# First projection of a two-layer encoder: units in pairs, square sums moved, second weight tile loaded earlier

## The reference, cut to what matters

```python
h = rms_norm(x, g_pre)                       # x * rsqrt(mean(x*x) + EPS) * g
proj = jnp.einsum('btd,de->bte', h, w_in)    # D = 1024 -> 2976 columns
qa, ka, va, cq, ckv, kr, gate = jnp.split(proj, SPLIT_AB, axis=-1)
```

## Time and profile before

| | |
|---|---|
| median of 3 runs | 2136.87 us (2136.51 to 2137.25) |
| profiled execution | 2129.73 us, span 2127.9 us |
| busy share: PE, PEld, DVE, ACT, POOL | 96%, 76%, 61%, 53%, 45% |
| DMA | 260.29 MB, 122 GB/s mean |

### The profile page before, as it was taken

The page is one execution under the profiler, slowest core; times in us unless marked ns, Lnnn a source line. Parts: engine busy times, 40 slices in busy tenths (PEclk is TensorE's granted clock), DMA queues, the critical chain, the costliest instruction groups (busy, mean ns, idle before and its releaser), DMA issues.

```text
span 2127.9 us, 25150 instructions
## 1 busy us (share of the span) xinstructions
PE 2041.6 (96%) x9334; PEld 1626.7 (76%) x9334; DVE 1287.6 (61%) x1922; ACT 1122.3 (53%) x1420; POOL 953.1 (45%) x477
## 2 busy tenths in 40 slices
PE   7999998999999999999997999999999999998997
PEld 5878876788888877777785777887777777775775
DVE  6232135326777766674568677524577887788454
ACT  7142234335666666664456444243677777777431
POOL 1222234334555555555001666423566666766401
PEclk9999999999999999999998999999999999999999
DMA  5133468527665555454335233261333333332534
GB/s 188 45 129 131 149 242 319 152 75 151 129 125 115 109 118 114 90 178 151 91 107 180 94 109 109 89 194 66 82 69 66 75 79 75 77 110 84 168 101 157
DMA packets 167434, 260.29 MB, mean 122 GB/s; under 512 B 75456, under 2 KB 84288, under 8 KB 167312
## 3 DMA queue, kind: packets, MB, share of 16 engines
q1 hardware_dynamic: 167312, 258.68, 42.5%
HBM read 160.72 MB, written 97.91 MB: 122 GB/s over the span
## 4 chain that ended last, share of the span: by engine, by line
PE 82%; DVE 10%; ACT 3%; issue 2%; DMA 2%; POOL 0%; SPq 0%; DVEq 0%; ACTq 0%
PE SA L1847 11%; PE OP L1891 9%; PE SA L473 5%; PE OP L473 5%; PE SM L1773 5%; PE OP L998 5%; PE SA L998 4%; PE OP L1898 4%; PE SM L1946 4%; PE SA L1946 3%; PE OS L473 3%; PE OS L1891 2%; PE OS L998 2%; PE SM L1769 2%; PE OS L1946 2%
## 5 line engine op out<-in xcount | busy, mean ns | idle before, releaser
L2295 POOL TENSOR_TENSOR c_PL<-c_PF,c_PH 128x1024 fp32r<-128x1024 f32 x128 | 308.8, 2418 | 151.8 <-ACT c_PH L2023 82.0
L2295 POOL TENSOR_TENSOR ab_PL<-ab_PF,ab_PH 128x1024 fp32r<-128x1024 f32 (+3 forms) x128 | 266.6, 2085 | 189.0 <-ACT ab_PH L2023 130.8
L2020 ACT ACTIVATE ab_PF<-SA 128x1024 f32<-128x1024 f32 (+3 forms) x160 | 143.6, 898 | 157.9 <-PE SA L1808 83.1
L2100 DVE TENSOR_REDUCE c_MH<-SM 128x1 f32<-128x512 f32 x256 | 171.8, 686 | 75.6 <-PE SM L1773 74.9
L2020 ACT ACTIVATE c_PF<-SA 128x1024 f32<-128x1024 f32 x160 | 164.0, 1025 | 93.7 <-PE SA L1847 93.3
L394 POOL TENSOR_TENSOR e_wl<-e_raw,e_wh 128x1024 fp32r<-128x1024 f32 (+1 forms) x31 | 73.6, 2375 | 217.7 <-ACT e_wh L539 217.7
L2023 ACT ACTIVATE c_PH<-c_PF 128x1024 fp32r<-128x1024 f32 x128 | 135.7, 1061 | 4.1
L1847 PE MATMUL SA<-c_Q,c_KA 128*128 128x512 f32 x320 | 129.4, 404 | 7.9 <-ACT c_PF L2020 7.9
L1773 PE MATMUL SM<-c_KA,c_Q 128*128 128x512 f32 x320 | 126.8, 398 | 4.4 <-DVE c_MH L2100 3.0
L1847 PE MATMUL SA<-c_Q,c_KB 72*128 72x512 f32 x320 | 128.5, 402 | 0.0
L2023 ACT ACTIVATE ab_PH<-ab_PF 128x1024 fp32r<-128x1024 f32 (+3 forms) x128 | 119.6, 935 | 4.0
(11 more groups left out here) (489 smaller groups left out, 5991.6 us busy)
## 6 DMA issues: line engine op xcount, KB each, us to landing
c_Q<-qC_hi SPq DMA_DIRECT2D x32, 384.0 KB, 4.9
e_raw<-in_w_tiles SPq DMA_DIRECT2D x20, 512.0 KB, 4.2
n_raw<-in_w_tiles SPq DMA_DIRECT2D x18, 512.0 KB, 3.8
e_XF<-in_xT SPq DMA_DIRECT2D x12, 512.0 KB, 10.9
silu_gate<-e_ta SPq DMA_DIRECT2D x24, 256.0 KB, 2.0
ab_Q<-qA_hi SPq DMA_DIRECT2D x16, 384.0 KB, 5.3
ab_G<-silu_gate SPq DMA_DIRECT2D x24, 256.0 KB, 3.6
ab_res<-in_xT SPq DMA_DIRECT2D x24, 256.0 KB, 2.9
```

The lines of the kernel that those rows point to most:

```text
L2020: nc.scalar.activation(used(PF[p], h, s), used(SA, h, s), ACT.Exp).then_inc(e_done, 1)
L2100: nc.vector.reduce_max(dst, src, axis=AX_X).then_inc(m_done, 1)
L2295: nc.gpsimd.tensor_tensor(used(PL[p], h, s), used(PF[p], h, s), used(PH[p], h, s).bitcast(F32), ALU.subtract).then_inc(p_lo[0], 1)
```

## The change

Six edits, all in `entry`:

1. **Idle products.** Ahead of everything TensorE multiplies the tile of ones by itself 14 times (128 columns) into a bank half that nothing reads.
2. **Second weight tile inside x.** Its load stands behind the first two loads of chunk 0, where it stood behind all four; ScalarE makes its wh between tile 1 and tile 2 of chunk 0, where it did so behind tile 7.
3. **Pairs.** Units 0 and 1, 2 and 3, 4 and 5 are made by `products_pair`: at step i the high-part products of tile i for the first unit, that of tile i-1 for the second, and four steps behind the products with low parts for both. In the third pair the second unit's wl and low products come last, behind square sum 0.
4. **Squares in places of their own.** All 24 squares keep a tile each (`x_squares`, `x_total`), in space that other tiles use later, so ScalarE waits for no add.
5. **Adds later.** VectorE's loop makes the 24 low parts with six adds of chunk 0 among them and the seventh ahead of the eviction of unit 0; chunk 1's seven adds come behind eviction 1, chunk 2's behind eviction 3.
6. **Square sums and roots later.** Sum 0 inside the third pair, sums 1 and 2 behind units 7 and 9; ScalarE's roots at n = 5, 8 and 10.

```diff
+    apart = [at(f"apart{i}", [P, CH], F32, REST + 18432 + 2048 * i) for i in range(9)]
+    x_squares = (apart[0:7], sh[0:4] + sl[0:3], ta + tb + apart[7:9])
+    x_total = (ssum[0], ssum[1], sl[3])
...
         load(0)
         sp.dma_start(gpre[0][:], A["gpre"][0]).then_inc(gain_in, 16)
-        load_x(0)
+        load_x(0, 0, 4)
         load(1)
+        load_x(0, 4, KT)
         load_x(1)
         load_x(2)
...
         def x_square_sum(c):
             pe.wait_ge(x_sum, (KT - 1) * (c + 1))
-            square_sum(c, ssum[c % 2][:])
+            square_sum(c, x_total[c][:])
...
+        def products_pair(n):
+
+            c = U[n][2]
+
+            def step(b, w, x, k, lo=False):
+                return nc.tensor.matmul(bank(n + b), w[b][:, k * P:(k + 1) * P], x[:, k, cols(c)],
+                                        start=(k == 0 and w is wh and not lo), stop=(lo and k == KT - 1))
+
+            def low(b, k):
+
+                pe.wait_ge(x_lo, c * KT + k + 1)
+                mm = step(b, wh, XL, k, True)
+                if k == KT - 1:
+                    mm.then_inc(mm_done, 1)
+
+            for i in range(KT + 4):
+                if i < KT:
+                    pe.wait_ge(x_hi, c * KT + i + 1)
+                    if n + i == 0:
+                        pe.wait_ge(w_hi, 1)
+                    step(0, wh, XH, i)
+                    if n + i == 0:
+                        pe.wait_ge(w_lo, 1)
+                    step(0, wl, XH, i)
+                if 1 <= i <= KT:
+                    if n + i == 1:
+                        pe.wait_ge(w_hi, 2)
+                    step(1, wh, XH, i - 1)
+                if i >= 4:
+                    if n + i == 4:
+                        pe.wait_ge(w_lo, 2)
+                    low(0, i - 4)
+                    if c < 2:
+                        step(1, wl, XH, i - 4)
+                        low(1, i - 4)
+            if c == 2:
+                x_square_sum(0)
+                for k in range(KT):
+                    step(1, wl, XH, k)
+                for k in range(KT):
+                    low(1, k)
...
+        pe.wait_ge(ones_set, 2)
+        for i in range(14):
+            nc.tensor.matmul(sums[1][:, 0:P], ones[:], ones[:], start=True, stop=True)
         for n in range(N):
-            if kind[n] == "value":
+            if n < 6:
+                if n % 2 == 0:
+                    products_pair(n)
+            elif kind[n] == "value":
...
-            if n in (0, 2, 4):
-                x_square_sum(n // 2)
+            if n in (7, 9):
+                x_square_sum(n // 2 - 2)
...
         def split_x(c):
             for k in range(KT):
+                if (c, k) == (0, 2):
+                    high_weights(1)
...
-                if k == 0:
-                    wait_count(act, total, c - 1)
-                else:
-                    wait_count(act, x_sum, (KT - 1) * c + max(0, k - 2))
-                out = ssum[c % 2] if k == 0 else sq[k % 2]
+                out = x_squares[c][k - 1] if k else x_total[c]
...
-        split_x(0)
-        high_weights(1)
-        split_x(1)
-        root(0, rstd[:, cols(0)], D)
-        split_x(2)
-        root(1, rstd[:, cols(1)], D)
+        for c in range(NC):
+            split_x(c)
         for n in range(N):
             for w in splits[n]:
                 high_weights(w)
+            if n in (5, 8, 10):
+                c = (n - 4) // 3
+                root(c, rstd[:, cols(c)], D)
...
-            if n == 2:
-                root(2, rstd[:, cols(2)], D)
...
-        split_x(0)
-        split_x(1)
-        split_x(2)
+        for c in range(NC):
+            for k in range(KT):
+                low_x(c, k)
+                if c > 0 and k in (1, 4, 7):
+                    add_square(0, 3 * c - 2 + k // 3)
         for n in range(N):
...
+            if n == 0:
+                add_square(0, KT - 1)
             evict(n)
+            if n in (1, 3):
+                for k in range(1, KT):
+                    add_square(n // 2 + 1, k)
```

More of the change, by code:

```diff
@@ L318, in load, with load_x @@
             sp.dma_start(dst, src).then_inc(raw_in[w % 2], 16)
-        def load_x(c):
-            for k in range(0, KT, 2):
+        def load_x(c, k0=0, k1=KT):
+            for k in range(k0, k1, 2):
                 sp.dma_start(XF[:, k:k + 2, cols(c)],
@@ L468, in products @@
                 for k in range(KT):
-                    if w == 0:
-                        pe.wait_ge(x_lo, c * KT + k + 1)
                     ks = slice(k * P, (k + 1) * P)
@@ L643, in vector, with low_x, add_square @@
     def vector(dve, between):
[L644 to L654, removed]
+        def low_x(c, k):
+            dve.wait_ge(x_sq, c * KT + k + 1)
+            dve.wait_ge(x_hi, c * KT + k + 1)
+            nc.vector.scalar_tensor_tensor(out=XL[:, k, cols(c)], in0=XF[:, k, cols(c)], scalar=gpre[0][:, k:k + 1],
+                                           in1=XH[:, k, cols(c)].bitcast(F32), op0=ALU.mult, op1=ALU.subtract
+                                           ).then_inc(x_lo, 1)
+        def add_square(c, k):
+            dve.wait_ge(x_sq, c * KT + k + 1)
+            wait_count(dve, x_sum, (KT - 1) * c + k - 1)
+            nc.vector.tensor_tensor(x_total[c][:], x_total[c][:], x_squares[c][k - 1][:], ALU.add
+                                    ).then_inc(x_sum, 1)
         def evict(n):
```

## The result

| | before | changed |
|---|---|---|
| median | 2135.74 us (20 runs, 2130.26 to 2143.22) | 2139.22 us (20 runs, 2135.49 to 2145.34) |
| ratio of the two | | 1.0022, interval 1.0013 to 1.0031 |
| profiled execution | 2129.73 us, span 2127.9 | 2136.39 us, span 2134.6 |
| busy PE, PEld, DVE, ACT, POOL | 96%, 76%, 61%, 53%, 45% | 96%, 77%, 60%, 53%, 45% |

The changed kernel is a little slower: the ratio is 4.7 us, 2.8 to 6.6. I had forecast +1.6 us and called it no change that can be told. The time fell inside my range, and partly by luck: my 2138.4 stands on a median of 2136.87 us from three runs, which twenty runs put at 2135.74. The size was three times mine, just over the 4.3 us that I had called measurable; 4.7 us on my own base would have been 2141.6, just above the range.

A forecast was written before the change was run, and what follows sets the result against it. From 21.59 us TensorE alone was taken to bound the kernel, after a front waiting on splits. Terms -5.05 + 1.72 + 4.9 = +1.6 us on a 2136.87 us median gave 2138.4 us, range 2133.4 to 2141.3.

The forecast's parts named there:

- The front: Dense pairs from 14.5 us: unit 6's first slot at 45.6 instead of 50.66, 5.05 us sooner.
- a front cold beyond 16 us: Rival: four products of the dense stretch at half speed, 0.9 us; with both falls 2142.2. Chance 0.11 shared with both falls.
- The reading of the clock column: Granted-clock column reads 1.00 also over half-speed first products, so product starts must tell: 0.43 us against 0.227.
- What guards unit 6: Before unit 6: wh until 42.5, wl until 45.0 at 2.37 us, first eviction ends 44.6; in time, counted 0.
- The late sums: Square sums 1 and 2 now behind units 7 and 9, after the mark: 2 x 0.86 = 1.72 us added.
- the two waits: TensorE stands still before units 8 and 10 for root and eviction: twice 2.45, 4.9 us added.
- Signs of being wrong: Waits missing, products behind them starting 0.43 us apart, or the span differing by more than unit 11 does.
- The clock: Rival: the clock falls to half speed at the two stalls, 1.45 us each; the forecast sum has 0.
- one fall: Rival: half speed behind one of the two stalls, giving 2139.9 us; chance 0.17.
- Behind unit 11 nothing is new: After unit 11 the change adds no time; unit 11 itself ends 1.6 us later than 83.47.
- No waits: Rival: root and eviction are hidden, so no stalls before units 8 and 10: -3.3 us, 2133.5; chance 0.08.
- a late weight tile: Rival: the second weight tile still lands at 13.2, tile 2 split 2.6 us later: 2140.9; chance 0.06.

The follow-up runs named there:

- the repeat: The changed kernel run once more with no edit: 2139.57 us, ratio 1.0022 to the kernel before.
- the kernel without idle products: The changed kernel without the fourteen idle products at its head: 2138.87 us, ratio 1.0025 to the kernel before.
- early sums: The changed kernel with square sum 1 behind sum 0, sum 2 behind unit 5, roots and adds earlier: 2135.08 us, in the second series 2134.87 us.
- Without the idle products as well: The changed kernel with square sums 1 and 2 issued early and the fourteen idle products removed: 2131.00 us, again 2133.67 us; ratios 0.9983 and 0.9989.
- without pairs: The changed kernel with units 0 to 5 made one by one, all else kept: 2143.20 us, ratio 1.0033 to the kernel before.
- the kernel with filled waits: The changed kernel with ten idle products behind each of square sums 1 and 2: 2139.17 us, ratio 1.0021 to the kernel before.
- Making wh late: The early sums kernel with the second weight tile loaded behind chunk 0's x and its wh made behind tile 7: one run, 2144.07 us.
- front filled: The early sums kernel with seven more idle products between the first pair's steps: 2134.44 us, ratio 0.9995 to the kernel before.
- idle products alone: The kernel before with only the fourteen idle products added at its head: 2133.81 us, ratio 0.9994 to the kernel before.
- Two by two between large products: Early sums without idle products, token scales spread two by two behind unit 11's first six k: 2134.21 us, ratio 0.9992 to the kernel before.

## Why the prediction was right, and where its size was not

- **The front: right.** -5.05 forecast, unit 6's first slot at 45.98 instead of 45.6, and at 45.65 in the repeat. x's first tile was split at 7.21, 0.7 sooner than in the earlier trace rows, and the weight tile landed 0.7 sooner than I took. What ate both: from 12.71 to 15.84 seven products take 3.13 us where 1.59 would do, 1.5 us. I had this among the rivals, as a front cold beyond 16 us, at 0.9; it was cold until 15.84 and cost more. I had expected the first products to be cold if anything was. They were at full speed, and the clock was down behind them, when the work became dense.
- **The reading of the clock column: wrong.** I said that it reads 1.00 also over products at half speed. In these profiles that holds only ahead of its first rise. In the kernel without idle products 0.43 us apart reads 1.00, and with them the same stretch reads 0.51 or 0.55. Elsewhere the column tells: 0.52 from 310 us in the profile before.
- **What guards unit 6: right.** wh was done at 42.8, wl went from 42.87 to 45.27, 2.40 us beside an eviction, as I took it, against 3.07. The first eviction started at 44.07. The rule of the Trainium skill (SBUF — State Buffer, Who interferes with whom) agrees on both sides: the 2.40 beside an eviction (first two rows below, GpSimd and VectorE), and at 12.08 three of VectorE's splits with two SBUF inputs that take 3.16 us beside GpSimd's wl (10.99 to 13.37), where three of 0.75 take 2.25. But that wl took 2.38 us, the same as beside an eviction: there VectorE paid, and not GpSimd as in the earlier trace rows.

```profile
42.87 2.40 POOL L398 TENSOR_TENSOR e_wl<-e_raw,e_wh 128x1024 fp32r<-128x1024 f32 x1 [29.50 <-ACT e_wh L589]
44.07 1.29 DVE L719 TENSOR_TENSOR e_LF<-SA,e_rstd 128x512 f32<-128x512 f32 x2 [6.02 <-ACT e_rstd L607]
```

```profile
10.99 2.38 POOL L398 TENSOR_TENSOR e_wl<-e_raw,e_wh 128x1024 fp32r<-128x1024 f32 x1 [3.17 <-ACT e_wh L589]
12.08 3.16 DVE L692 SCALAR_TENSOR_TENSOR e_XL<-e_XF,gpre,e_XH 128x512 fp32r<-128x512 f32 x3 [1.71 <-ACT e_apart L600]
```

- **The late sums, 1.72, and the two waits, 4.9: right.** Both waits stand where I had put them, 2.16 us idle each. Taking them away gave 4.8 ± 0.6 us. Unit 11 came 1.62 us late in the execution whose clock held at the waits.
- **Signs of being wrong: two of three came.** In the first profile products behind both waits start 0.43 us apart, and the execution is 6.7 us longer than that of the kernel before where unit 11 is 5.2 later.
- **The clock: the term that was mis-sized.** My sum has 0 for it. The measured 4.8 us (2139.58 - 2134.74) are 3.2 over my 1.6. With early sums my sum would be -5.05 + 1.72 = -3.3, and 0.0 was measured: 3.4 over, without any wait. So the excess is not bound to the waits. Without the idle products as well it is 1.1 ± 0.7 (-2.2 measured), and there the half-speed time is that of the kernel before (65.7 against 66.9), where the two others have 9 to 11 us more. The excess goes with half-speed time, and with early sums 3.1 of its 3.4 us lie behind unit 11.
- **The falls at the waits: seen, but not shown to cost mean time.** I gave 0.17 to one fall and 0.11 to both, or to one with a cold front. In the profiles of kernels that have the two waits unfilled (changed twice, without idle products, without pairs) the clock fell behind five of eight (two, none, two, one), at 1.6 us each. I had priced one at 1.45, so the price was right and the chance too low. By it two waits would cost some 2 us of clock in a mean execution. But taking both away gave 4.8 ± 0.6 us, their own length, where 4.9 + 2 would be 6.9: what falls at the waits in one kernel seems to fall elsewhere in the other. My own count in the profile before gave four of nine, and I talked it down because mine follow dense units. That was no reason: the units ahead of both waits are dense, and it fell behind them. The Trainium skill (TensorE: Matmul & The Clock Gate, Why this matters for your kernels) puts the idle gap that throttles above 2.16 us, and by it nothing falls here. The falls at 60.04 and 75.85 disagree with it.
- **A third fall that I did not have.** Behind the token scales the clock fell in the profiled execution at a price of 3.11 us. It did so in nine of eleven profiles of kernels with a changed front and the scales in a block (not in the changed kernel's repeat, nor without pairs), and in neither of the two with the old front. "Behind unit 11 nothing is new" was wrong in time, though not in instructions: with early sums 3.1 us are lost there. What decides it is not shown.
- **The rest of the size.** The sum had 1.6; the front adds 0.0 to 0.4. The half-speed time of the changed kernel is 9.1 us longer (76.0 against 66.9), some 3.4 of them the front's, unrecorded before. The other 5.7 cost 1.8 us at the mean slope of 0.31, and 2.6 at the price behind the first wait, where 3.5 us at half speed (60.04 to 63.53) cost 1.61. Together 3.4 to 4.6 us, an estimate, against 4.7 measured. How the falls of a mean execution are shared among the places isn't measured, and why a kernel with a changed front has more of them stays open. In the kernel with filled waits two of them were gone in the profile and no time was gained that could be told, so this account is the likely one and not a settled one.
- **Rivals that fell.** No waits (-3.3) and a late weight tile did not happen. Making wh late cost 6.0 us for 6.9 by one profile, near the price that I had for it.

## What to carry to other kernels

A reduction whose result gates evictions (square sum, root, scale) must be issued as many units ahead as its own chain is long. Here the sum stood directly ahead of the product that needed its result, and pushing it "out of the way" cost more (4.8 us) than the dense front had brought (3.1 us at unit 11, by the profile with early sums). Issued early instead, and without the idle products, it gave the one version that beats both kernels (0.9983 and 0.9989). Falls of the clock follow some waits of 2 us (five of eight here), but don't read their price from one profile: here the mean time gained by taking the waits away was their own length. When effects are some 0.2%, read each execution's mean granted clock beside its time before believing a difference, compare on one chip, and pay for repeats.

## What the runs showed of the hardware

- Half-speed time varies between executions of one kernel and goes with most of their spread: correlation 0.89 over 97 executions, 0.31 us of time for each us. Behind the first wait, where TensorE alone sets the pace, it is 1.61 us for 3.5, or 0.46 us for each us.
- Warm-up products of ones do not fix the clock of what follows. After a pause of 1.40 us (changed kernel) the next product was at full speed, after 2.12 us (front filled) at half speed, and after 2.92 us (idle products alone) too. But after 2.45 us (the changed kernel again) and 2.71 us (early sums, second series) it was at full speed, so the length of the pause does not decide it. And the clock that was up at 7.99 was down at 12.71.

```profile
8.40 0.50 PE L472 MATMUL SA<-e_XH,e_wh 128*128 128x512 f32 x1 [2.45 <-ACT e_XH L597]
```

- Twelve products of one column, 24 passes, take 2.91 us, more than twelve of 512 columns (12 x 0.2267 = 2.72). Two by two between large products they take 0.77 us a pair with what they cost the one behind.
- Open stay three things: whether the idle products cost anything with early sums (2.3 ± 0.7 us over all series, 1.0 ± 0.9 on one chip), what makes the clock fall behind the token scales and more often behind a changed front, and whether a fall at a wait is an extra one or one that would have come elsewhere.
